# Eight instead of six pieces of the first expert loaded ahead of the ring, and the buffer clearing moved behind the first copy

## The chip, the cores and the metric

The kernel runs on one core of one Trainium2 chip, as one program. The metric is the device time of one execution in microseconds; for the kernel before it is the median of three runs.

## The reference

A decoder trunk of two layers over 256 rows of 1024 float32 values. Layer 0 is latent attention with eight heads and a dense SwiGLU mixer of 2816 columns. Layer 1 is sliding-window attention (16 heads, sinks, a bias by distance) and a mixture of experts. Only the mixture matters for the change:

```python
logits = xn @ w_router                       # 8 experts
top_val, top_idx = lax.top_k(logits, 2)      # each row goes to two of them
hg, hu = xs @ w_gate[e], xs @ w_up[e]        # 1024 x 3584 each
hh = silu(hg) * hu * gate
out += hh @ w_down[e]                        # 3584 x 1024
```

The weights of the eight experts are 8 x 3 x 1024 x 3584 float32 values, 352 MB of the 413 MB that the kernel reads. A final RMS norm follows.

## The kernel before

One block holds a program for each engine. SyncE (SP) issues nearly all weight loads, in one fixed order, into a ring of 28,672 columns in SBUF. In the dense layers the ring is seven slots of 4096 columns. In the mixture it is 16 places (`LAPS`) of one piece each: a piece is 1792 columns (`PIECE`, 896 KB, 128 partitions). An expert has 48 pieces: for each half of its 3584 columns and each of eight k rows one gate and one up piece (m = 0 to 31), then 16 of the down projection (m = 32 to 47), which are loaded in pairs. Piece m lies in place m % 16. Before a load, `room_for` makes SP wait until TensorE has read what lay there. With the first expert these are, for m < 16, the dense weights that the place covers: places of pieces 10 to 12 want the third output product of the attention (`swo_mm` 3), those of 13 and later the fourth. For m = 16 to 31 the count `gu_read` (one per k row that TensorE has read, starting from 1) is waited for, or `gu_mm` for the eighth row of a half. The down pair m = 32, 33 wants the first row of half 1 read.

TensorE takes one item (an expert with its gathered rows) at a time: eight k rows of half 0 (`products(i, 0, k)`), eight of half 1 with transposes and the scatter of the item before between them, the down rows of both halves, and the gather for the next item. An item of at most 64 rows takes the narrow path, one of up to 96 the wide path. The order in which the experts come mixes both. ScalarE (ACT) makes silu of the gate quarters of a half into `sg` (L974), VectorE (DVE) multiplies it with the up quarter into `hh` (L2098), and TensorE begins quarter c of half 1 only when quarter c of half 0 is out of PSUM (`hh_ready`, L1546).

Six pieces of the first expert don't wait for a place in the ring. SP loads them into SBUF that is free before the first item begins: AHEAD_A (m = 30, 31) and AHEAD_B (22, 23) into the end of the arena after the attention's last transposes, and AHEAD_C (26, 27) into xT2 and xT after the router. GpSimd (POOL) copies them into their ring places when these come free (`take_ahead`, L752 to 757, run for B, C, A in this order: the fourth k row of the first half read, the sixth, the eighth). B lies where the transposed hidden values `hhT` are written later, and so ACT waits for both copies of B before it enters its item loop (L1024 to 1025). The places of pieces that come ahead are skipped in SP's order.

Earlier, POOL clears the pads of `slots` and `gates`, and the whole of `ysb`, `sgt` and `hh` (L746 to 750). DVE waits for all five (`cleared`, L1998), and uses the still unused `hh` as scratch room for ranking the experts. After its last copies POOL loads the final gain `gfin` over the room of C (L764).

Of the kernel before, what the change touches and what calls it, by code (L numbers as in the profile page):

```python
# [37 lines left out]
P = 128  # L38
# [12 lines left out]
AH, KVH, HD = 16, 2, 64  # L51
# [8 lines left out]
NE, DFE = 8, 3584  # L60
# [9 lines left out]
ITEMS_MAX = NE * SWEEPS  # L70
# [5 lines left out]
PIECE = HALF_F  # L76
LAPS = 16
# [50 lines left out]
class Semaphores:  # L128
    def __init__(self, sem):
# [120 lines left out]
        self.ahead_loaded_a = sem("ahead_loaded_a")  # L250
        self.ahead_loaded_b = sem("ahead_loaded_b")
        self.ahead_loaded_c = sem("ahead_loaded_c")
        self.gu_read = sem("gu_read")
        self.gu_mm = sem("gu_mm")
        self.sg_ready = sem("sg_ready")
# [21 lines left out]
def build(nc, x, positions, w_in, g_q, g_kv, w_uq, w_ukv, w_o, kv_g, kv_w, kv_b, swa_w_q, swa_b_q,  # L277
          swa_sinks, swa_w_o, swa_b_o, rel_bias, g_attn, g_ffn, f_gate, f_up, f_down, w_router,
          e_gate, e_up, e_down, g_final, consts, out):
    with ExitStack() as ctx:  # L280
# [18 lines left out]
        xT = sb("xT", [P, KD, S])  # L299
        xT2 = sb("xT2", [P, KD, S])  # L300
# [12 lines left out]
        n_items = sb("n_items", [P, 2], I32)  # L313
        wide = sb("wide", [P, ITEMS_MAX], I32)
        order = sb("order", [P, NE], I32)
        ranks = sb("ranks", [P, 8, NE])
        slots = sb("slots", [P, TT, ITEMS_MAX + 1])
        gates = sb("gates", [P, TT, ITEMS_MAX + 1])
# [89 lines left out]
        selg = carve(TT * SLOTS, "p (t n) -> p t n", t=TT)  # L408
        sgt = carve(TT * P, "p (t n) -> p t n", t=TT)
        xgT = carve(KD * SLOTS, "p (k n) -> p k n", k=KD)  # L410
        hh = carve(HALF_F)
        sg = carve(2 * CH, "p (a n) -> p a n", a=2)
        ysb = carve(D)
        early = 12288 - 4 * PIECE
        assert used[0] <= early
        used[0] = early
        hhT = carve(2 * TILES * SLOTS, "p (a j n) -> p a j n", a=2, j=TILES)
        below = hh[:, 0:NE * NE].rearrange("p (a b) -> p a b", a=NE)
        at_place = hh[:, NE * NE:2 * NE * NE].rearrange("p (a b) -> p a b", a=NE)
        terms = hh[:, 2 * NE * NE:5 * NE * NE].rearrange("p (v a b) -> p v a b", v=3, a=NE)  # L420
        gfin = xT2[:].rearrange("p k n -> p (k n)")[:, 0:D]

        AHEAD_B = {LAPS + 6: arena[:, early:early + PIECE], LAPS + 7: arena[:, early + PIECE:early + 2 * PIECE]}
        AHEAD_C = {LAPS + 10: xT2[:].rearrange("p k n -> p (k n)")[:, 0:PIECE], LAPS + 11: xT[:].rearrange("p k n -> p (k n)")[:, 0:PIECE]}
        AHEAD_A = {LAPS + 14: arena[:, early + 2 * PIECE:early + 3 * PIECE], LAPS + 15: arena[:, early + 3 * PIECE:early + 4 * PIECE]}
        assert used[0] <= early + 2 * PIECE

# [180 lines left out]
        @block.sync  # L608
        def _(sp):
            sp.dma_start(h[:, 0, :], x[0, 0:P, :]).then_inc(s.x_loaded0, 16)  # L610
            sp.dma_start(ident, consts[:, C_ID:C_ID + P]).then_inc(s.ident_loaded, 16)
            sp.dma_start(h[:, 1, :], x[0, P:2 * P, :]).then_inc(s.x_loaded1, 16)
            for n, (name, src, k, cols, _, _) in enumerate(stream):
                old = earlier_fill(n, slot_of[n])
                if old is not None:
                    sp.wait_ge(stream[old][4], stream[old][5])
                sp.dma_start(w_of(name), src).then_inc(slot_landed[slot_of[n]], 16)
                if name == "win_q":
                    sp.dma_start(cst[:, C_ID + P:C_N], consts[:, C_ID + P:C_N]).then_inc(s.consts_loaded, 16)

            def piece_of_expert(m, expert):
                kind, half, part = pieces[m]
                if kind == "d":
                    return ed[:, expert, half, part * PIECE:(part + 1) * PIECE]
                return (eg if kind == "g" else eu)[:, expert, part, half * HALF_F:(half + 1) * HALF_F]

            def room_for(i, m, first):

                if m < LAPS:
                    if not first:  # L630
                        sp.wait_ge(s.down_mm, i * (2 * TILES) + (last_down_row(m + 2 * LAPS) + 2 - 2 * TILES))
                        return
                    for sl in dense_under(m):
                        if sl >= 5:
                            sp.wait_ge(*used_up(NU - 1))
                        else:
                            sp.wait_ge(*stream[earlier_fill(DENSE, sl)][4:6])
                    return
                kind, half, k = pieces[m - LAPS]
                if kind == "u":  # L640
                    return
                if k < KD - 1:
                    sp.wait_ge(s.gu_read, i * (2 * KD - 2) + (half * (KD - 1) + k + 2))
                else:
                    sp.wait_ge(s.gu_mm, i * 8 + (4 * half + 5))

            def load_item(i, expert, first):
                for m in range(NP):
                    if first and m == 10:
                        sp.wait_ge(s.spT_mm, AH)  # L650
                        for ma, room in AHEAD_A.items():
                            sp.dma_start(room, piece_of_expert(ma, expert)).then_inc(s.ahead_loaded_a, 16)
                        for ma, room in AHEAD_B.items():
                            sp.dma_start(room, piece_of_expert(ma, expert)).then_inc(s.ahead_loaded_b, 16)
                    if first and m == LAPS:
                        sp.wait_ge(s.swo_mm, 4)
                        sp.wait_ge(s.router_mm, 2)
                        for ma, room in AHEAD_C.items():
                            sp.dma_start(room, piece_of_expert(ma, expert)).then_inc(s.ahead_loaded_c, 16)
                    if first and (m in AHEAD_A or m in AHEAD_B or m in AHEAD_C):  # L660
                        continue
                    room_for(i, m, first)
                    if pieces[m][0] != "d":
                        sp.dma_start(piece(m), piece_of_expert(m, expert)).then_inc(s.piece_landed[m % LAPS], 16)
                    elif m % 2 == 1:
                        _, half, part = pieces[m]
                        sp.dma_start(whole[:, place(m - 1):place(m - 1) + 2 * PIECE],
                                     ed[:, expert, half, (part - 1) * PIECE:(part + 1) * PIECE]).then_inc(s.piece_landed[(m - 1) % LAPS], 16)

            load_item(0, 0, True)  # L670
            sp.wait_ge(s.counts_ready, 1)
            sp.wait_ge(s.order_ready, 1)
            with sp.Fori(1, NE) as i:
                load_item(i, sp.value_load(order[0:1, bass.ds(i, 1)], min_val=0, max_val=NE - 1), False)

            items = sp.value_load(n_items[0:1, 0:1], min_val=NE, max_val=ITEMS_MAX)
            for sweep in range(1, SWEEPS):
                with sp.If(items > sweep * NE):
                    with sp.Fori(0, NE) as e:
                        load_item(e + sweep * NE, sp.value_load(order[0:1, bass.ds(e, 1)], min_val=0, max_val=NE - 1), False)  # L680
                with sp.Else():
                    sp.nop()
            rows = out[0].rearrange("(t p) d -> t p d", p=P)
            sp.wait_ge(s.row_done, 1)
            sp.dma_start(rows[0], xn[:, 0, :]).then_inc(s.out_stored, 16)
            sp.wait_ge(s.row_done, 2)
            sp.dma_start(rows[1][:, 0:512], xn[:, 1, 0:512]).then_inc(s.out_stored, 16)
            sp.wait_ge(s.out_stored, 48)
# [3 lines left out]
        def _(pool):  # L692
# [53 lines left out]
            pool.wait_ge(s.swo_mm, 2)  # L746
            for v in (slots[:, :, ITEMS_MAX:ITEMS_MAX + 1], ):
                nc.gpsimd.memset(v, -1.0).then_inc(s.cleared, 1)
            for v in (gates[:, :, ITEMS_MAX:ITEMS_MAX + 1], ysb[:], sgt[:], hh[:]):
                nc.gpsimd.memset(v, 0.0).then_inc(s.cleared, 1)  # L750
            rstd_rows()
            def take_ahead(rooms, landed, free, count):  # L752
# [3 lines left out]
                for m, room in rooms.items():  # L756
                    nc.gpsimd.tensor_copy(piece(m), room).then_inc(s.piece_landed[m % LAPS], 16)

            take_ahead(AHEAD_B, s.ahead_loaded_b, s.gu_read, 5)
            take_ahead(AHEAD_C, s.ahead_loaded_c, s.gu_read, 7)  # L760
            take_ahead(AHEAD_A, s.ahead_loaded_a, s.gu_mm, 5)
            for m in AHEAD_C:
                pool.wait_ge(s.piece_landed[m % LAPS], 32)
# [9 lines left out]
        def _(act):  # L773
# [247 lines left out]
                act.copy(ysb[NARROW:SLOTS, 512:1024], ps[SLOTS:P, DOWN_BANK, :]).then_inc(s.act_chain, 1)  # L1021
                act.copy(ysb[0:SLOTS, 0:512], ps[0:SLOTS, DOWN_BANK, :]).then_inc(s.y_ready_a, 1)

            for m in AHEAD_B:  # L1024
                act.wait_ge(s.piece_landed[m % LAPS], 32)

            with act.Fori(0, items) as i:
# [640 lines left out]
        def _(dve):  # L1668
# [326 lines left out]
            add_out(3, s.swo_mm, s.h_attn1, SWO_BANK)  # L1995
            evac_hT(1, 1)
            mean_squares(3, 1, D)
            dve.wait_ge(s.cleared, 5)  # L1998
            for q in (s.sel_ready, s.selg_ready, s.hh_ready, s.y_ready_v, s.xgT_ready_v, s.h_added):
                dve.sem_inc(q, 1)  # L2000

            lg, mask, top, idx = (rt[:, :, 8 * n:8 * n + 8] for n in range(4))
# [80 lines left out]
            def dve_item(i, narrow):  # L2083
# [21 lines left out]
                else:  # L2105
                    dve.tensor_copy(ysb[0:NARROW, 512:768], ps[0:NARROW, DOWN_BANK + 1, 0:LASTQ]).then_inc(s.y_last, 1)
                    dve.tensor_copy(ysb[0:NARROW, 768:1024], ps[64:64 + NARROW, DOWN_BANK + 1, 0:LASTQ]).then_inc(s.y_ready_v, 1)

            with dve.Fori(0, items) as i:
                many = dve.value_load(wide[0:1, bass.ds(i, 1)], min_val=0, max_val=1)  # L2110
                with dve.If(many > 0):
                    dve_item(i, False)
                with dve.Else():
                    dve_item(i, True)
# [32 lines left out]
```

## Time and profile before

| | us |
|---|---|
| median of three runs | 1241.17 (1240.88 to 1242.95) |
| the profiled execution | 1240.27 |
| its span | 1238.5 |
| TensorE busy | 1201.4 (97%) |
| VectorE busy | 313.4 (25%) |
| ScalarE busy | 252.4 (20%) |
| GpSimd busy | 40.6 (3%) |

The profile divides the span into 40 slices of 31 us. In the slices from about 433 us on, the mixture, both TensorE and the DMA engines stand at nine tenths or more; before, the DMA engines have slices of three to six tenths. Busy times of TensorE are those of pipelined matmuls with modelled ends. "issue" is time in which an engine waited for nothing that the profile shows. The clock granted to TensorE is given as a share of its full speed.

### The profile page before, as it was taken

What the parts mean: (1) busy time and instruction counts of PE and PEld (TensorE: products, weight loads), DVE (VectorE), ACT (ScalarE), POOL (GpSimd) and SP (SyncE); (2) the same over time, 40 slices, a digit from 0 to 9 for tenths busy, and PEclk for the clock granted to TensorE, in tenths of its full rate; (3) what the DMA queues carried; (4) which work ended last, traced back from release to release, by engine and by line L of the source; (5) the groups of instructions that cost most, each with busy time, mean ns of one, the idle gap of its engine ahead of it and who ended that gap; (6) DMA issues with size and microseconds to landing.
All of it is one profiled execution on the core that took longest, in us unless ns stands there. A gap on an engine that the chain in (4) does not pass through costs nothing.

```text
span 1238.5 us, 20372 instructions
## 1 busy us (share of the span) xinstructions
PE 1201.4 (97%) x8373; PEld 616.4 (50%) x8374; DVE 313.4 (25%) x710; ACT 252.4 (20%) x485; POOL 40.6 (3%) x60
## 2 busy tenths in 40 slices
PE   7999999999999999899999999999999999999996
PEld 4865777778765534334333433443343343334333
DVE  3364676667272311010001002001100100100011
ACT  2252433333263111011021011102101101110111
POOL 2100000000201120000000000000000000000001
PEclk9999999999999999999999999999999999999999
DMA  9613654336635799999999999999999999999994
GB/s 342 231 69 123 217 204 144 129 126 237 241 119 201 318 381 423 419 422 426 419 419 427 418 419 424 422 418 420 427 417 419 426 421 418 423 424 400 421 426 166
DMA packets 73309, 413.19 MB, mean 334 GB/s; under 512 B 6622, under 2 KB 11996, under 8 KB 64780
## 3 DMA queue, kind: packets, MB, share of 16 engines
q1 hardware_dynamic: 71744, 410.41, 81.9%
q8 instruction: 66, 1.08, 0.4%
q0 software_dynamic: 944, 1.29, 0.4%
q10 hardware_dynamic: 540, 0.29, 0.1%
q14 instruction: 15, 0.12, 0.0%
HBM read 410.91 MB, written 1.05 MB: 333 GB/s over the span
## 4 chain that ended last, share of the span: by engine, by line
PE 84%; DMA 7%; DVE 3%; issue 2%; ACT 2%; POOL 0%; ACTq 0%; DVEq 0%; POOLq 0%; SPq 0%
PE ps L1548 19%; PE ps L1528 11%; PE ps L1523 6%; PE ps L1506 6%; PE ps L1620 5%; DMA ring<-in_moe_w_up 4%; PE ps L1221 4%; PE ps L1217 4%; PE ps L1218 4%; PE ps L1510 3%; PE ps L1583 3%; PE ps L1393 2%; PE ps L1603 2%; PE ps L1183 2%; DMA ring<-in_moe_w_down 2%
## 5 line engine op out<-in xcount | busy, mean ns | idle before, releaser
L1548 PE MATMUL ps<-ring,arena 128*64 128x448 f32 x640 | 250.4, 545 | 7.0 <-issue 4.3
L1549 PE MATMUL ps<-ring,arena 128*64 128x448 f32 x640 | 250.5, 545 | 0.0
L1528 PE MATMUL ps<-ring,arena 128*32 128x448 f32 x1152 | 162.1, 539 | 0.0
L1548 PEld LDWEIGHTS ps<-ring,arena 128*64 128x64 f32 x640 | 84.7, 137 | 153.1 <-issue 139.2
L1529 PE MATMUL ps<-ring,arena 128*32 128x448 f32 x384 | 160.0, 539 | 0.0
L1620 PE MATMUL ps<-ring,arena 128*64 128x512 f32 x280 | 124.4, 595 | 0.3 <-DMA ring<-in_moe_w_down 0.3
L1621 PE MATMUL ps<-ring,arena 128*64 128x512 f32 x280 | 124.4, 595 | 0.0
L2098 DVE TENSOR_TENSOR arena<-arena,ps 64x448 f32<-64x448 f32 (+1 forms) x64 | 38.5, 613 | 303.0 <-ACT arena L974 153.6
L1523 PE MATMUL ps<-ring,arena 128*32 128x448 f32 x768 | 91.2, 542 | 5.4 <-DVE arena L2098 4.0
L1528 PEld LDWEIGHTS ps<-ring,arena 128*32 128x32 f32 x1152 | 50.9, 110 | 90.9 <-issue 90.9
L1844 DVE TENSOR_TENSOR w_lo<-ring,w_hi 128x2048 fp32r<-128x2048 f32 x33 | 75.5, 2291 | 60.0 <-ACT w_hi L860 58.6
L1506 PE MATMUL ps<-ring,arena 128*32 128x512 f32 x504 | 87.2, 593 | 0.0
L860 ACT CAST w_hi<-ring 128x2048 fp32r<-128x2048 f32 x33 | 62.9, 1908 | 114.2 <-PE ps L1221 114.2
L1507 PE MATMUL ps<-ring,arena 128*32 128x512 f32 x168 | 86.0, 594 | 0.0
L1549 PEld LDWEIGHTS ps<-ring,arena 128*64 128x64 f32 x640 | 84.8, 137 | 0.0
L1620 PEld LDWEIGHTS ps<-ring,arena 128*64 128x64 f32 x280 | 37.0, 137 | 73.0 <-issue 71.6
L1217 PE MATMUL ps<-w_hi,xT_hi 128*128 128x512 f32 (+1 forms) x192 | 71.6, 380 | 0.0
L1218 PE MATMUL ps<-w_hi,xT_lo 128*128 128x512 f32 (+1 forms) x192 | 70.1, 372 | 0.0
L2080 DVE TENSOR_TENSOR h<-h,ps 128x512 f32<-128x512 f32 x36 | 24.7, 687 | 167.2 <-PE ps L1583 167.2
L985 ACT COPY arena<-ps 128x320 f32<-128x320 f32 (+3 forms) x48 | 21.8, 454 | 207.8 <-PE ps L1603 207.8
L1510 PE MATMUL ps<-ring,arena 128*32 128x256 f32 x672 | 51.7, 379 | 0.0
L1523 PEld LDWEIGHTS ps<-ring,arena 128*32 128x32 f32 x768 | 23.8, 109 | 50.5 <-issue 40.8
(301 smaller groups left out, 1428.7 us busy)
## 6 DMA issues: line engine op xcount, KB each, us to landing
ring<-in_moe_w_down SPq DMA_DIRECT2D x64, 1792.0 KB, 24.2
ring<-in_moe_w_gate SPq DMA_DIRECT2D x125, 896.0 KB, 18.2
ring<-in_moe_w_up SPq DMA_DIRECT2D x125, 896.0 KB, 19.3
ring<-in_ffn_w_gate SPq DMA_DIRECT2D x5, 2048.0 KB, 7.8
ring<-in_ffn_w_up SPq DMA_DIRECT2D x5, 2048.0 KB, 8.2
ring<-in_ffn_w_down SPq DMA_DIRECT2D x5, 2048.0 KB, 7.9
ring<-in_mla_w_o SPq DMA_DIRECT2D x2, 2048.0 KB, 25.6
ring<-in_swa_w_q SPq DMA_DIRECT2D x2, 2048.0 KB, 8.5
```

The source lines that it names most:

```text
L1217: pe.matmul(out, lhs[0][:, k, c], rhs_hi[:, k, :], start=(first and k == 0), stop=False)
L1218: pe.matmul(out, lhs[1][:, k, c], rhs_hi[:, k, :], start=False, stop=False)
L1506: pe.matmul(ps[32 * j:32 * j + 32, bank, :], thirds[j], left, start=first, stop=last)
L1507: pe.matmul(ps[SLOTS:P, bank, :], thirds[2], right, start=first, stop=last)
L1510: mm = pe.matmul(ps[q:q + 32, bank + 1, 0:LASTQ], thirds[j], right[:, cols:cols + LASTQ], start=first, stop=last)
L1523: pe.matmul(ps[q:q + 32, 4 + c // 2, 0:CH], thirds[j], wg[:, (c + e) * CH:(c + e + 1) * CH], start=first, stop=last)
L1528: pe.matmul(ps[32 * j:32 * j + 32, c, 0:CH], thirds[j], wu[:, c * CH:(c + 1) * CH], start=first, stop=last)
L1529: mm = pe.matmul(ps[SLOTS:P, c, 0:CH], thirds[2], wg[:, c * CH:(c + 1) * CH], start=first, stop=last)
L1548: pe.matmul(ps[0:NARROW, c, 0:CH], lhs, wu[:, cols], start=(k == 0), stop=(k == KD - 1))
L1549: mm = pe.matmul(ps[64:64 + NARROW, c, 0:CH], lhs, wg[:, cols], start=(k == 0), stop=(k == KD - 1))
L1620: pe.matmul(ps[0:NARROW, DOWN_BANK, :], lhs, w[:, 0:512], start=first, stop=last)
L1621: mm = pe.matmul(ps[64:64 + NARROW, DOWN_BANK + 1, :], lhs, w[:, 512:1024], start=first, stop=last)
```

## The change

Pieces 24 to 31, the last four k rows of half 1, are now those that come ahead, in four pairs: D (24, 25), B (26, 27), C (28, 29), A (30, 31). Pieces 22 and 23 go through the ring. D lies in the arena from column `HH0`, where `hh`, `sg` and most of `ysb` are later. SP issues it at m = 13, after the attention's eighth product with the values (`spv_mm` 8). POOL takes D first, when the fifth k row is read, waits for its own two copies, clears `hh` and `ysb`, and goes on with B, C and A. ACT waits for the copies of D and of B before its loop, and DVE for the clearing of `hh`. The scratch views for ranking get a tensor of their own.

```diff
+        scratch = sb("scratch", [P, 5 * NE * NE])
...
+        HH0 = used[0]
         hh = carve(HALF_F)
         sg = carve(2 * CH, "p (a n) -> p a n", a=2)
         ysb = carve(D)
+        assert used[0] - HH0 >= 2 * PIECE
...
-        below = hh[:, 0:NE * NE].rearrange("p (a b) -> p a b", a=NE)
+        below = scratch[:, 0:NE * NE].rearrange("p (a b) -> p a b", a=NE)
...
-        AHEAD_B = {LAPS + 6: arena[:, early:early + PIECE], LAPS + 7: arena[:, early + PIECE:early + 2 * PIECE]}
-        AHEAD_C = {LAPS + 10: xT2[:].rearrange("p k n -> p (k n)")[:, 0:PIECE], LAPS + 11: xT[:].rearrange("p k n -> p (k n)")[:, 0:PIECE]}
+        AHEAD_D = {LAPS + 8: arena[:, HH0:HH0 + PIECE], LAPS + 9: arena[:, HH0 + PIECE:HH0 + 2 * PIECE]}
+        AHEAD_B = {LAPS + 10: arena[:, early:early + PIECE], LAPS + 11: arena[:, early + PIECE:early + 2 * PIECE]}
+        AHEAD_C = {LAPS + 12: xT2[:].rearrange("p k n -> p (k n)")[:, 0:PIECE], LAPS + 13: xT[:].rearrange("p k n -> p (k n)")[:, 0:PIECE]}
...
+                    if first and m == 13:
+                        sp.wait_ge(s.spv_mm, AH // 2)
+                        for ma, room in AHEAD_D.items():
+                            sp.dma_start(room, piece_of_expert(ma, expert)).then_inc(s.ahead_loaded_d, 16)
...
-            for v in (gates[:, :, ITEMS_MAX:ITEMS_MAX + 1], ysb[:], sgt[:], hh[:]):
+            for v in (gates[:, :, ITEMS_MAX:ITEMS_MAX + 1], sgt[:]):
                 nc.gpsimd.memset(v, 0.0).then_inc(s.cleared, 1)
...
-            take_ahead(AHEAD_B, s.ahead_loaded_b, s.gu_read, 5)
-            take_ahead(AHEAD_C, s.ahead_loaded_c, s.gu_read, 7)
+            take_ahead(AHEAD_D, s.ahead_loaded_d, s.gu_read, 6)
+            for m in AHEAD_D:
+                pool.wait_ge(s.piece_landed[m % LAPS], 32)
+            nc.gpsimd.memset(hh[:], 0.0).then_inc(s.rows_cleared, 1)
+            nc.gpsimd.memset(ysb[:], 0.0).then_inc(s.y_ready_v, 1)
+            take_ahead(AHEAD_B, s.ahead_loaded_b, s.gu_read, 7)
+            take_ahead(AHEAD_C, s.ahead_loaded_c, s.gu_read, 8)
             take_ahead(AHEAD_A, s.ahead_loaded_a, s.gu_mm, 5)
...
-            for m in AHEAD_B:
+            for m in (*AHEAD_D, *AHEAD_B):
                 act.wait_ge(s.piece_landed[m % LAPS], 32)
...
-            dve.wait_ge(s.cleared, 5)
-            for q in (s.sel_ready, s.selg_ready, s.hh_ready, s.y_ready_v, s.xgT_ready_v, s.h_added):
+            dve.wait_ge(s.cleared, 3)
+            for q in (s.sel_ready, s.selg_ready, s.hh_ready, s.xgT_ready_v, s.h_added):
...
+            dve.wait_ge(s.rows_cleared, 1)
             with dve.Fori(0, items) as i:
```

## Rows read from the trace of the kernel before

**Rows 1.** Page, part 2: DMA engines' busy tenths in 40 slices.
```profile
DMA  9613654336635799999999999999999999999994
```
**Rows 2.** Stretches: us, busy of PE, PEld, DVE, ACT, POOL, PEclk, DMA share, GB/s.
```profile
444.00:445.00 1.00, 1.00 (x8) 0.52 (x5) 0.00 (x0) 0.00 (x0) 0.77 (x2) 1.00 0.35 144
445.00:446.00 1.00, 1.00 (x7) 0.48 (x8) 0.00 (x0) 0.42 (x1) 0.00 (x0) 1.00 0.49 102
...
452.00:500.00 48.00, 48.00 (x242) 19.93 (x242) 6.71 (x13) 5.15 (x13) 0.00 (x0) 1.00 1.01 424
500.00:800.00 300.00, 294.25 (x2162) 115.83 (x2158) 29.44 (x55) 35.45 (x72) 0.00 (x0) 0.99 1.01 422
```
**Rows 3.** Line 664 (gate and up loads), 520 to 1240 us: issue to landing.
```profile
DMA to landing us min/median/max: 11.1/22.2/30.2
```
**Rows 4.** Waits of PE from 500 us on: total, times, longest.
```profile
PE ps L1548 <- issue: 3.3, 1, 3.3
...
PE ps L1523 <- DMA ring<-in_moe_w_up: 1.4, 2, 0.8
```
**Rows 5.** SP's issues in order of time: start, duration, line, target and source.
```profile
395.63 0.43 SPq L664 DMA_DIRECT2D ring<-in_moe_w_gate  x1
402.97 0.33 SPq L664 DMA_DIRECT2D ring<-in_moe_w_up  x1
...
431.78 0.33 SPq L664 DMA_DIRECT2D ring<-in_moe_w_gate  x1
...
437.80 0.33 SPq L664 DMA_DIRECT2D ring<-in_moe_w_gate  x1
...
444.60 0.33 SPq L667 DMA_DIRECT2D ring<-in_moe_w_down  x1
```
**Rows 6.** Line 664, the load issued at 419.8 alone: issue to landing.
```profile
DMA to landing us min/median/max: 5.5/5.5/5.5
```
**Rows 7.** Line 667, the down pair issued at 444.6 alone: issue to landing.
```profile
DMA to landing us min/median/max: 8.7/8.7/8.7
```
**Rows 8.** POOL in order of time, 428 to 445 us.
```profile
428.92 3.29 POOL L757 COPY ring<-arena 128x1792 f32<-128x1792 f32 x2 [21.06 <-PE ps L1549]
434.92 3.30 POOL L757 COPY ring<-xT 128x1792 f32<-128x1792 f32 x2 [2.71 <-PE ps L1549]
...
444.18 0.59 POOL L764 DMA_DIRECT2D xT<-in_g_final  x1
```
**Rows 9.** POOL's groups by shape, 390 to 400 us: busy us, mean ns.
```profile
L750 POOL MEMSET arena<- 128x1792 f32 x1 | 1.6, 1597 | 0.0
L750 POOL MEMSET arena<- 128x1024 f32 x1 | 1.0, 951 | 0.0
```
**Rows 10.** ACT's sequencer, lines 1025 and 971: ns, first and last start us.
```profile
L1025 ACTq EVENT_SEMAPHORE  x1: 17/17/17, 432.2 to 432.2; - x1
...
L971 ACTq FUSED_REGOPS  x1: 47/47/47, 433.2 to 433.2; - x1
```
**Rows 11.** ACT in order of time, 436 to 442 us.
```profile
438.69 1.28 ACT L974 ACT_TABLE_LOAD   x1 [22.12 <-PE ps L1549]
439.99 0.97 ACT L974 ACTIVATE arena<-ps 64x448 f32<-64x448 f32 x2
```
**Rows 12.** The chain that ended last, 436 to 446 us: start, duration.
```profile
440.66 0.62 DVE arena L2098
...
441.33 0.59 PE ps L1548
```
**Rows 13.** PE in order of time, 501 to 512 us.
```profile
506.34 1.00 PE L1548 MATMUL ps<-ring,arena 128*64 128x448 f32 x1 [3.32 <-issue]
...
509.26 0.54 PE L1548 MATMUL ps<-ring,arena 128*64 128x448 f32 x1
509.63 0.54 PE L1548 MATMUL ps<-ring,arena 128*64 128x448 f32 x1
```
**Rows 14.** A stretch of that time, columns as in rows 2.
```profile
507.00:508.00 1.00, 1.00 (x6) 0.35 (x4) 0.00 (x0) 0.00 (x0) 0.00 (x0) 0.50 1.04 430
```

More of the change, by code:

```diff
@@ L252, in __init__ @@
         self.ahead_loaded_c = sem("ahead_loaded_c")
+        self.ahead_loaded_d = sem("ahead_loaded_d")
+        self.rows_cleared = sem("rows_cleared")
         self.gu_read = sem("gu_read")
@@ L417, in build @@
         hhT = carve(2 * TILES * SLOTS, "p (a j n) -> p a j n", a=2, j=TILES)
-        below = hh[:, 0:NE * NE].rearrange("p (a b) -> p a b", a=NE)
-        at_place = hh[:, NE * NE:2 * NE * NE].rearrange("p (a b) -> p a b", a=NE)
-        terms = hh[:, 2 * NE * NE:5 * NE * NE].rearrange("p (v a b) -> p v a b", v=3, a=NE)
+        below = scratch[:, 0:NE * NE].rearrange("p (a b) -> p a b", a=NE)
+        at_place = scratch[:, NE * NE:2 * NE * NE].rearrange("p (a b) -> p a b", a=NE)
+        terms = scratch[:, 2 * NE * NE:5 * NE * NE].rearrange("p (v a b) -> p v a b", v=3, a=NE)
         gfin = xT2[:].rearrange("p k n -> p (k n)")[:, 0:D]
-        AHEAD_B = {LAPS + 6: arena[:, early:early + PIECE], LAPS + 7: arena[:, early + PIECE:early + 2 * PIECE]}
-        AHEAD_C = {LAPS + 10: xT2[:].rearrange("p k n -> p (k n)")[:, 0:PIECE], LAPS + 11: xT[:].rearrange("p k n -> p (k n)")[:, 0:PIECE]}
+        AHEAD_D = {LAPS + 8: arena[:, HH0:HH0 + PIECE], LAPS + 9: arena[:, HH0 + PIECE:HH0 + 2 * PIECE]}
+        AHEAD_B = {LAPS + 10: arena[:, early:early + PIECE], LAPS + 11: arena[:, early + PIECE:early + 2 * PIECE]}
+        AHEAD_C = {LAPS + 12: xT2[:].rearrange("p k n -> p (k n)")[:, 0:PIECE], LAPS + 13: xT[:].rearrange("p k n -> p (k n)")[:, 0:PIECE]}
         AHEAD_A = {LAPS + 14: arena[:, early + 2 * PIECE:early + 3 * PIECE], LAPS + 15: arena[:, early + 3 * PIECE:early + 4 * PIECE]}
@@ L659, in load_item @@
                             sp.dma_start(room, piece_of_expert(ma, expert)).then_inc(s.ahead_loaded_c, 16)
-                    if first and (m in AHEAD_A or m in AHEAD_B or m in AHEAD_C):
+                    if first and (m in AHEAD_A or m in AHEAD_B or m in AHEAD_C or m in AHEAD_D):
                         continue
```

## The prediction, made before the changed kernel was run

> **What bounds the kernel now.** I read the slices first [rows 1]: from the fourteenth or so on the DMA engines are full, and before it they are not. The stretches say the same in numbers [rows 2]: 424 and 422 GB/s at a share of 1.01 from 452 us on, with nothing left to win per byte, but 0.35 and 0.49 in the two microseconds after 444. Then I asked whether the queue runs dry later. It does not: after 520 us no gate or up load landed sooner than 11.1 us after its issue, median 22.2 [rows 3], where one that found the queue empty took 5.5 [rows 6]. So from the first pair of down pieces, issued at 444.60 [rows 5], to the last landing, the DMA engines work without a hole. TensorE is nearly as full, and keeps within a microsecond of them: it waits for a gate or up piece only twice, 1.4 us in all, at most 0.8 [rows 4]. The end is therefore set by when that unbroken stream begins, plus its bytes. TensorE may be late by up to about 0.8 us at those places for nothing.
>
> **The change part by part.**
>
> Bytes. Two more pieces of 896 KB are loaded early. At 422 GB/s a piece takes 2.17 us [rows 2], so 4.3 us of work leave the stretch after 420 us. But which work? The loads issued at 437.80 (28, 29) now come ahead, as do 24 and 25 of 431.78 [rows 5]; 22 and 23 come back, at 428.8. All these lie before the hole, and the next load in SP's order is the down pair, whose place is free only when TensorE has read the first k row of half 1 (444.60). DMA already idles there. Taking 4.3 us away in front of a hole that a wait for room makes only widens it: from about 441 instead of 445. Gain: 0. Every transfer behind the hole is in both kernels. At the other end, if none of the hole counted, it would be the whole 4.3.
>
> The new loads themselves. SP stands waiting between 395.63 and 402.97 [rows 5] for the fourth output product; D is issued in this gap, since the eighth product with the values is ahead of the third output product in TensorE's program. Its two issues (0.43 us each at the row's duration) hide there. They push pieces 13 to 15 and C back by 4.3 us of DMA time, and none is wanted before half 0 reaches its seventh k row near 434.9. Piece 16, issued at 419.76 into an empty queue, has the engines to itself in both kernels. Pieces 22 and 23, now by ring, are the seventh and eighth in that queue: 425.3 + 7 x 2.17 = 440.5. They are read no sooner than three k rows (of 3.0 us, below) after 441.3, at 450. Cost 0.
>
> POOL. This is where I find the price. B's copies began at 428.92 (four k rows read) and C's at 434.92 (six); a k row is 3.0 us, so D's begin at 431.92 (five). Then in order: two copies 3.3 (to 435.2), the clearing of hh 1.6 and of ysb 0.95 [rows 9] (to 437.8, with about 0.1 for the wait on its own copies), and B's two copies 3.3 [rows 8], to 441.2. B's own condition, six rows, was met long before. C's copies follow to 444.5, A's to 447.8; their pieces are the seventh and eighth k row of half 1, read 18 us after it begins, so these hide.
>
> ACT. Before, it passed its wait for B at 432.2 and was ready inside the loop at 433.2 [rows 10]: 1.0 us of register reads and a branch, 5 us ahead of need. The first silu had to wait for TensorE alone: table load at 438.69, silu at 439.99, 1.3 us later [rows 11]. Now the wait ends at 441.2, the loop is entered by 442.2, the table load starts some 0.15 later and the silu at 443.65: 3.65 us late. The table load is behind the same wait and can't be done meanwhile. The chain shows that nothing covers this [rows 11, 12]: silu 439.99, multiply 440.66, first matmul of half 1 at 441.33. TensorE has nothing else in its program there. It restarts at 445.0.
>
> TensorE's clock. Half 0 ends at 440.8 (C's copies at 434.92 plus two k rows, less 0.1 that POOL takes to start); TensorE now stands until 445.0, 4.2 us instead of 0.5. The only comparable stop is at 503: 3.32 us idle, then matmuls at a granted clock of 0.50, which is 1.2 GHz [rows 13, 14]. The four steps from 506.34 to 509.26 took 2.92 us where four at full clock take 4 x 0.37 = 1.5: a loss of 1.4. Bounds for this stop: 0 if the clock doesn't fall, 1.7 if the slow stretch meets it fully. I take 1.4, since this stop is longer. (The Trainium skill, "TensorE: Matmul & The Clock Gate", section "What's actually happening", says that throttled is the default state and activity releases it. By that rule the restart is slow; the rows at 506 agree. With the rule the first down pair is 5.05 us late, without it 3.65.)
>
> DVE. The wait for the cleared hh ends near 436.9, before its first multiply at 440.66: 0. Own scratch room, fewer clears at 393 and one semaphore increment less: all before 411 or beside other work, between -0.1 and 0.1. The first scatter wants ysb only after four k rows of half 1, past 453: 0. I see no cost of copies beside the multiplies: the multiply of 440.66 ran beside a copy in 0.62.
>
> The stream. The down pair is issued at 444.60 + 3.65 + 1.4 = 449.65. Before, it landed 8.7 us after issue [rows 7]; alone it would have taken 5.5 + 2.17 = 7.7, and the 1.0 more went to the gfin load, issued 0.4 us ahead of it [rows 8]. Now gfin goes out at 447.8, 1.9 us ahead, and has most of its bytes through in the hole: I give back 0.9 of the 1.0 at best, nothing at worst. Stream late by 5.05 - 0.9 = 4.15. Without a clock drop the pair goes at 448.25, gfin 0.5 ahead as before, nothing given back: 3.65. Later pairs wait for room on the same late TensorE; their backlog then was small, which could keep up to 0.9 more. TensorE, 5.05 late, loses 0.8 where it used to wait for DMA: 4.25, no more than the stream. The sum lies between 3.65 and 5.05; I take 4.0, between the two clock cases.
>
> Against the profile's own time: span 1238.5 + 4.0 = 1242.5, execution 1240.27 + 4.0 = 1244.3. The median of the runs was 0.9 above the profiled one, so 1241.17 + 4.0 = 1245.2.
>
> **The rivals.**
>
> The stream is shortened (faster). If the early bytes counted, all landings after 450 would come 4.3 us sooner and the time be 1236.9. For it: DMA full for 770 us, and TensorE waiting for it twice. Against: the hole after 444 [rows 2], made by room and not by bytes. It decides only if the down pair finds its place sooner, and nothing makes TensorE read sooner. Between this and nothing lies the 1.0 us of gfin: 1240.2.
>
> The late silu is hidden (no change), 1241.2. For it: TensorE has 0.8 us to spare later and 3.3 us of a stop at 503 [rows 4] that a late start might swallow if it is tied to a time and not to TensorE's position. Against: slack of TensorE doesn't help a DMA stream whose first load is late. It wants DMA to have a second hole, and rows 3 show none.
>
> A deeper loss. The clock falls and stays low longer, and the pairs behind the first keep the whole 5 us or more: 1246.2 to 1247.
>
> **How the numbers follow.** Late silu with a stream 3.6 to 4.4 us later: 0.65. Deeper loss: 0.16. Partly hidden, 1242 to 1244: 0.08. No change: 0.07. Faster: 0.04. From 1242.6 to 1247.2 holds some 0.85 of it. What a measurement can tell from no change is 0.2%, 2.5 us, so slower needs over 1243.65: 0.65 + 0.16 and half of the partly hidden, 0.85; same 0.11; faster 0.04.
>
> **What would show it.** In the changed trace: POOL's order copy x2, memset, memset, copy x6 without a break from 431.9 to 447.8; ACT's table load at 442.3 and not 438.7; TensorE idle some 4 us before the first matmul of half 1, with a granted clock of 0.5 near 445 to 448; the first down load issued at 448 to 450; DMA share near 0 from 441 to 449 apart from gfin, and 1.01 from then on at the same GB/s; the last landing later by what the first down pair was late. Wrong would be: the silu still at 440 (the wait or the order on POOL misread); the silu late and the end unmoved (a hole in the stream that I missed); the first down load near 444.6 with an earlier end (the bytes counted after all).

## The result, and the profile after

The changed kernel takes 1246.34 us, median of seven runs (1244.9 to 1247.63), against 1241.17 (1240.79 to 1242.95, seven runs): ratio 1.004, interval 1.003 to 1.005, 5.2 us slower. The profiled execution took 1247.63 us with a span of 1245.8; it is the slowest of the seven, so the two profiles differ by 7.4 and not 5.2.

POOL in order of time, 425 to 452 us of the changed kernel (start, duration, line):

```profile
433.12 3.29 POOL L767 COPY ring<-arena 128x1792 f32<-128x1792 f32 x2 [24.65 <-PE ps L1564]
436.54 1.59 POOL L772 MEMSET arena<- 128x1792 f32 x1
438.06 0.95 POOL L773 MEMSET arena<- 128x1024 f32 x1
438.96 3.30 POOL L767 COPY ring<-arena 128x1792 f32<-128x1792 f32 x2
442.20 3.30 POOL L767 COPY ring<-xT 128x1792 f32<-128x1792 f32 x2
445.45 3.30 POOL L767 COPY ring<-arena 128x1792 f32<-128x1792 f32 x2
448.70 0.59 POOL L779 DMA_DIRECT2D xT<-in_g_final  x1
```

ACT, and then TensorE, in order of time in the same stretch:

```profile
443.50 1.28 ACT L989 ACT_TABLE_LOAD   x1 [24.67 <-issue]
444.79 0.97 ACT L989 ACTIVATE arena<-ps 64x448 f32<-64x448 f32 x2
...
```

```profile
441.42 0.54 PE L1563 MATMUL ps<-ring,arena 128*64 128x448 f32 x1
...
446.13 1.01 PE L1563 MATMUL ps<-ring,arena 128*64 128x448 f32 x1 [4.17 <-DVE arena L2113]
...
446.94 0.95 PE L1563 MATMUL ps<-ring,arena 128*64 128x448 f32 x1
...
447.68 0.95 PE L1563 MATMUL ps<-ring,arena 128*64 128x448 f32 x1
...
451.42 0.58 PE L1563 MATMUL ps<-ring,arena 128*64 128x448 f32 x1
```

POOL's ten memory operations, eight copies and two clears, now run on without a break, and the first six of them stand in front of the end of ACT's wait for B. (Each matmul of L1563, the up half of a step, has one of L1564, the gate half, beside it; those lines are left out.) The silu comes at 444.79 instead of 439.99 [rows 11]. TensorE stands 4.17 us, and its matmuls then begin every 0.75 us instead of 0.37 until 451.4. SP's issues, and the stretches (columns as in rows 2):

```profile
396.73 0.71 SPq L664 DMA_DIRECT2D arena<-in_moe_w_gate  x1
397.48 0.89 SPq L664 DMA_DIRECT2D arena<-in_moe_w_up  x1
403.59 0.33 SPq L674 DMA_DIRECT2D ring<-in_moe_w_up  x1
...
452.05 0.33 SPq L677 DMA_DIRECT2D ring<-in_moe_w_down  x1
```

```profile
441.00:445.00 4.00, 0.96 (x6) 0.14 (x2) 0.00 (x0) 1.49 (x2) 4.00 (x3) 0.96 0.01 4
445.00:449.00 4.00, 2.87 (x8) 1.00 (x10) 2.29 (x4) 1.84 (x4) 4.00 (x4) 0.50 0.00 0
449.00:453.00 4.00, 4.00 (x17) 1.57 (x15) 0.00 (x0) 0.20 (x1) 0.29 (x1) 0.69 0.38 131
453.00:500.00 47.00, 47.00 (x241) 19.94 (x239) 6.72 (x13) 5.80 (x15) 0.00 (x0) 1.00 1.00 408
500.00:800.00 300.00, 294.39 (x2152) 115.93 (x2148) 29.44 (x55) 34.42 (x68) 0.00 (x0) 0.99 1.01 422
```

D's loads hide in SP's gap. The first down pair goes out at 452.05 instead of 444.60, after 8 us in which the DMA engines move almost nothing (share 0.01, then 0.00). From 500 us on everything is as before: 1.01 and 422 GB/s, at a new offset. From 415 us on TensorE waits even less for gate and up pieces than in [rows 4]: once, 0.2 us.

Part of the 7.45 us between the two issues isn't the change's. The first product of item 0 starts at 417.69 here and at 416.49 in the profile of before; its start lies between 415.15 and 418.04 over all thirteen profiles of this study, in both kinds of kernel. So I count from that start. The down products of the two kernels, with the start of the first and the last of them:

```profile
L1620 PE MATMUL ps<-ring,arena x280: 592/592/644, 472.7 to 1224.8; 128*64 128x512 f32 x140
```

```profile
L1635 PE MATMUL ps<-ring,arena x280: 592/592/644, 480.1 to 1232.1; 128*64 128x512 f32 x140
```

Before: first down load 444.60 - 416.49 = 28.1 us after the start, last down product 1224.8 - 416.5 = 808.3. Changed: 34.4 and 814.4. The load is 6.3 late, the end 6.1. The same for all kernels, with the medians:

| kernel | silu | first down load | last down product | median, and of before beside it |
|---|---|---|---|---|
| before | 23.5 | 28.1 | 808.3 | |
| the change | 27.1 | 34.4 | 814.4 | 1246.34, 1241.17 |
| the change again | 27.1 | 34.1 | 814.4 | 1246.02, 1240.84 |
| B's wait later | 23.5 | 28.1 | 809.1 | 1241.71, 1242.26 |
| clears behind B | 24.8 | 29.4 | 809.5 | 1241.97, 1242.26 |
| ysb behind B | 26.2 | 32.5 | 812.5 | 1245.72, 1241.70 |
| kept busy | 27.1 | 31.7 | 811.8 | 1243.59, 1240.84 |
| before, ACT late | 28.7 | 34.9 | 815.1 | 1247.39, 1242.26 |
| four ahead | 23.5 | 28.1 | 809.4 | 1241.89, 1242.26 |
| eight, better order | 22.2 | 27.3 | 807.7, 807.5 | 1240.80, 1241.70; 1240.33, 1240.84 |
| six, same repairs | 22.2 | 27.3 | 807.7 | 1240.99, 1241.70 |
| primed alone | 22.2 | 27.3 | 808.7 | 1241.89, 1241.70 |

The columns are us from the start of item 0's first product to: the first silu, the issue of the first down pair, the start of the last down product. The end comes 780.0 to 781.4 us after the first down load in every row; it takes the longest, 781.0 to 781.4, in B's wait later, four ahead and primed alone. Each offset is from one profile. Against the one profile of before (1240.27, 0.9 under its median) the ends are 0.1 to 1.7 us later than the medians say, in all rows but the second run of the better order. So that profile was probably a short execution, also behind item 0's start; a single profile can't show it.

### The profile page after: what moved, and what is told of

Read it like the earlier page. It is cut to its first block, busy times and chain, and to the rows that moved or that the text cites. A ratio compares the mean times of both kernels' runs of the same rounds, so it can differ in the third digit from the quotient of the medians.

```text
span 1245.8 us, 20376 instructions
## 1 busy us (share of the span) xinstructions
PE 1207.1 (97%) x8373; PEld 615.5 (49%) x8374; DVE 313.6 (25%) x710; ACT 252.4 (20%) x485; POOL 43.7 (4%) x62
## 4 chain that ended last, share of the span: by engine, by line
PE 88%; DVE 3%; DMA 3%; issue 2%; ACT 2%; POOL 1%; ACTq 0%; POOLq 0%; DVEq 0%
PE ps L1563 19%; PE ps L1543 10%; PE ps L1635 9%; PE ps L1521 6%; PE ps L1538 5%; PE ps L1236 4%; PE ps L1232 4%; PE ps L1233 4%; PE ps L1525 3%; PE ps L1598 3%; PE ps L1618 3%; PE ps L1512 3%; PE ps L1408 2%; PE ps L1198 2%; DMA ring<-in_moe_w_up 2%
## 5 line engine op out<-in xcount | busy, mean ns | idle before, releaser
L1563 PE MATMUL ps<-ring,arena 128*64 128x448 f32 x640 | 254.7, 552 | 9.5 <-DVE arena L2113 6.3
L1564 PE MATMUL ps<-ring,arena 128*64 128x448 f32 x640 | 254.8, 553 | 0.0
L1563 PEld LDWEIGHTS ps<-ring,arena 128*64 128x64 f32 x640 | 85.8, 139 | 158.3 <-issue 140.9
L1543 PEld LDWEIGHTS ps<-ring,arena 128*32 128x32 f32 x1152 | 48.0, 110 | 93.6 <-issue 93.6
L1564 PEld LDWEIGHTS ps<-ring,arena 128*64 128x64 f32 x640 | 86.0, 139 | 0.0
L2095 DVE TENSOR_TENSOR h<-h,ps 128x512 f32<-128x512 f32 x36 | 24.8, 688 | 169.8 <-PE ps L1598 169.8
L1538 PEld LDWEIGHTS ps<-ring,arena 128*32 128x32 f32 x768 | 22.5, 110 | 50.7 <-issue 41.5
```

The lines of the kernel that those rows point to most:

```text
L1538: pe.matmul(ps[q:q + 32, 4 + c // 2, 0:CH], thirds[j], wg[:, (c + e) * CH:(c + e + 1) * CH], start=first, stop=last)
L1543: pe.matmul(ps[32 * j:32 * j + 32, c, 0:CH], thirds[j], wu[:, c * CH:(c + 1) * CH], start=first, stop=last)
L1563: pe.matmul(ps[0:NARROW, c, 0:CH], lhs, wu[:, cols], start=(k == 0), stop=(k == KD - 1))
L1564: mm = pe.matmul(ps[64:64 + NARROW, c, 0:CH], lhs, wg[:, cols], start=(k == 0), stop=(k == KD - 1))
```

## The experiments

### The wait for B taken out of the way

```diff
-            for m in (*AHEAD_D, *AHEAD_B):
+            for m in AHEAD_D:
                 act.wait_ge(s.piece_landed[m % LAPS], 32)
...
+                    if half == 0:
+                        for m in AHEAD_B:
+                            act.wait_ge(s.piece_landed[m % LAPS], 32)
                     for n in range(3):
                         hhT_evac(i, half, n, narrow)
```

> The changed kernel with ACT's wait for the copies of B taken from ahead of its item loop to ahead of the first transposed hidden values; it waits for D alone before the loop. Theory (the late silu makes the loss, and the early bytes are worth nothing): first silu back at about 440, first down load at about 444.6 to 445.2, time within 1 us of before, 1240.2 to 1242.2. Rival 1 (the two more pieces do shorten the stream once nothing else is late): 1236.9. Rival 2 (the loss comes from D itself, its room, loads or copies, not from the wait): still 1244 to 1247.

1241.71 us (1240.56 to 1242.49) against 1242.26 of before beside it, ratio 0.9998 (0.9989 to 1.0007). ACT, and SP:

```profile
438.25 1.28 ACT L989 ACT_TABLE_LOAD   x1 [21.06 <-PE ps L1567]
439.54 0.97 ACT L989 ACTIVATE arena<-ps 64x448 f32<-64x448 f32 x2
```

```profile
444.15 0.33 SPq L677 DMA_DIRECT2D ring<-in_moe_w_down  x1
```

With the start at 416.04 both stand exactly where before has them: silu 23.5 after it, down load 28.1. All the rest of the change is in this kernel. The bytes that are gone from the ring's queue only widen the hole in front of the down load, as two of its stretches show:

```profile
439.00:440.00 1.00, 1.00 (x8) 0.29 (x4) 0.00 (x0) 0.99 (x3) 1.00 (x1) 1.00 0.06 22
...
443.00:444.00 1.00, 1.00 (x6) 0.14 (x2) 0.00 (x0) 0.00 (x0) 1.00 (x2) 1.00 0.00 0
```

In before the DMA share was still 0.95 from 443 to 444 us. So the loss hangs on this wait, and the bytes gained nothing that the interval (1.1 us to either side) would show: 1236.9 is excluded.

### The clears behind B's copies

```diff
-            nc.gpsimd.memset(hh[:], 0.0).then_inc(s.rows_cleared, 1)
-            nc.gpsimd.memset(ysb[:], 0.0).then_inc(s.y_ready_v, 1)
             take_ahead(AHEAD_B, s.ahead_loaded_b, s.gu_read, 7)
+            nc.gpsimd.memset(hh[:], 0.0).then_inc(s.rows_cleared, 1)
+            nc.gpsimd.memset(ysb[:], 0.0).then_inc(s.y_ready_v, 1)
```

> The changed kernel with the clearing of hh and ysb put behind the copies of B instead of ahead of them, so that B is copied 2.6 us sooner. Theory: B copied by 438.5, silu at about 441.0, 1.0 us late, TensorE stands 1.5 us, its clock stays; the down load 1.0 late: 1241.6 to 1243.0. Rival (the clock falls or not with the mere order, the size of the delay being secondary): 1245 or more. Rival (bytes): 1237.9.

1241.97 (1241.39 to 1242.83), ratio 0.9997 (0.9988 to 1.0006). TensorE's wait, and a stretch behind it:

```profile
PE ps L1563 <- DVE arena L2113: 1.8, 1, 1.8
```

```profile
444.00:446.00 2.00, 2.00 (x12) 0.74 (x12) 1.14 (x2) 0.49 (x1) 2.00 (x2) 1.00 0.00 0
```

The silu is 1.3 us late, TensorE stands 1.8 us at full clock, and in the trace the down load is 1.3 late and the end 1.2; in the runs this small a loss doesn't show, and is 0.7 us at most by the interval. That is less than the 1.0 us that I expected. The rival with a fallen clock is out.

### Only the clearing of ysb behind B

```diff
             nc.gpsimd.memset(hh[:], 0.0).then_inc(s.rows_cleared, 1)
-            nc.gpsimd.memset(ysb[:], 0.0).then_inc(s.y_ready_v, 1)
             take_ahead(AHEAD_B, s.ahead_loaded_b, s.gu_read, 7)
+            nc.gpsimd.memset(ysb[:], 0.0).then_inc(s.y_ready_v, 1)
```

> The changed kernel with only the clearing of ysb (0.95 us) put behind the copies of B. Silu 2.7 us late, TensorE stands some 3.3 us, as long as at 503, where the clock fell. Theory (delay plus clock): if the clock falls for 3.4 us or more, stream 2.7 + 1.4 or more late, 3.5 to 5 us over before; if it stays up, 1.5 to 2.7 over. Rival (in proportion to the delay alone, no clock): 1.5 to 2.7 over before in all runs, and one level of times.

1245.72 (1245.08 to 1246.32), ratio 1.0033 (1.0021 to 1.0045): 4.0 us. Stretches of this kernel:

```profile
445.00:446.00 1.00, 1.00 (x4) 0.35 (x6) 0.84 (x2) 1.00 (x2) 1.00 (x2) 0.60 0.00 0
446.00:448.00 2.00, 2.00 (x8) 0.73 (x6) 0.69 (x2) 0.04 (x1) 2.00 (x2) 0.50 0.00 0
448.00:449.00 1.00, 1.00 (x6) 0.32 (x4) 0.00 (x0) 0.00 (x0) 0.95 (x2) 0.69 0.00 0
```

The silu is 2.7 us late and TensorE stands 3.3 us, until 444.91. Its clock falls 0.3 us after it has started again, and is low for 3.4 us; in the changed kernel it is low for 6.8. The down load is 4.4 late. Against the kernel with both clears behind B the silu is 1.4 us later and the down load 3.1; in the runs the two kernels lie some 4 us apart, each with an interval of over 1 us to either side. The loss is not in proportion to the delay: 1.7 us of the 3.1 are matmuls at half pace. That the clock fell is read from one profile; the six runs, all 3.4 us or more over the median of before beside them (1241.70), fit it, and none is at the 1.5 to 2.7 that the expectation gave for a clock that stays up.

### TensorE kept busy while it waits

```diff
+                    if k == 0 and half == 1 and c == 0:
+                        with pe.If(i < 1):
+                            for _ in range(4):
+                                keep_busy(5, 512)
```

> The changed kernel, with four matmuls on constants (some 0.86 us each, into a bank that nobody reads) that TensorE runs in the first item alone, between half 0 and the wait for the first quarter of half 1. ACT and POOL are as late as in the changed kernel, but TensorE stands some 0.7 us instead of 4.2. Theory (the loss is the late silu plus the slow clock after the standstill): clock stays at full, first down load 3.6 to 4 us late instead of 6 to 7, stream 3.5 late: 2 to 3 us under the changed kernel run beside it. Rival (the loss beyond the late silu is something else, a restart of the DMA queue or of the ring): within 0.7 us of the changed kernel.

1243.59 (1242.18 to 1245.31, 11 runs), ratio 1.0020 (1.0011 to 1.0029); the changed kernel beside it 1246.02. TensorE:

```profile
442.24 3.70 PE L1464 MATMUL ps<-cst 128*128 128x512 f32 x8
446.49 0.59 PE L1569 MATMUL ps<-ring,arena 128*64 128x448 f32 x1 [0.54 <-DVE arena L2119]
...
446.91 0.54 PE L1569 MATMUL ps<-ring,arena 128*64 128x448 f32 x1
...
447.29 0.54 PE L1569 MATMUL ps<-ring,arena 128*64 128x448 f32 x1
```

The four matmuls on constants, whose result nobody reads, are the eight records of the first line. The silu is as late as in the changed kernel (27.1), and POOL's order the same. Matmuls follow every 0.37 us, and the down load is 3.6 late instead of 6. So, by the medians, 2.4 us of the 5.2 are the clock's, and 2.75 the late silu's. The highest run here (1245.31) lies under the lowest of the changed kernel (1245.44); the size of the 2.4 is known to about 2 us, by the two intervals.

### The change again

> The changed kernel as it is, beside the others on the same chip: 4 to 5.5 us over before, with the clock at 1.2 GHz for 3.4 or 6.8 us from about 444 us on. Rival (the first result was in part the chip or the day): under 3 us over before.

1246.02 (1245.44 to 1246.73), ratio 1.0043 (1.0029 to 1.0057): 5.2 us, as the first time. TensorE stands 4.18 us, and six steps of its matmuls and part of a seventh go at half pace, for 4.8 us.

### Before, with ACT late and nothing else

```diff
-            for m in AHEAD_B:
+            for m in (*AHEAD_B, LAPS + 14):
                 act.wait_ge(s.piece_landed[m % LAPS], 32)
```

> The kernel before, six pieces as they were, with nothing but one more wait of ACT ahead of its loop: for the first copy of A, which ends at 442.6. Theory: silu at about 445.05, 5.05 us late; first down load 5 to 8 us late with the clock at 1.2 GHz for a stretch; 1246 to 1249. Without a fall of the clock 1245.5. Rival (the loss of the change comes from D's loads and copies, or from 7 to 8 us less of DMA work in the right place): under 1243.

1247.39 (1246.91 to 1248.12), ratio 1.0042 (1.0029 to 1.0056). Its waits of PE from 415 us on:

```profile
PE ps L1548 <- DVE arena L2098: 7.9, 5, 5.7
```

Six pieces, no D, no late clears, and a loss as soon as ACT is late: silu 5.2 late, down load 6.8, end 6.8 in the trace, 5.1 us in the runs. This is the other half of the proof: a late ACT is sufficient. It isn't a copy of the changed kernel, since the silu is later than there (5.2 against 3.6) for the same loss in the runs; of TensorE's slow time, 442.7 to 449.5, about half lies in the standstill, and the matmuls lose 1.7 us by it instead of 2.7.

### Four pieces ahead

```diff
-        AHEAD_C = {LAPS + 10: xT2[:].rearrange("p k n -> p (k n)")[:, 0:PIECE], LAPS + 11: xT[:].rearrange("p k n -> p (k n)")[:, 0:PIECE]}
+        AHEAD_C = {}
...
-            take_ahead(AHEAD_C, s.ahead_loaded_c, s.gu_read, 7)
```

> The kernel before with pair C (26, 27) not ahead but by its turn through the ring: four pieces ahead instead of six. Theory (a hole of 2 to 3.4 us stands between the last of half 1 and the first down pair, which the 4.3 us more fill first): stream late by 4.3 less the hole, 1 to 2.3 us: 1242.2 to 1243.5. Rival (each piece counts in full): 1245.5. Rival (no piece counts): 1241.2.

1241.89 (1240.42 to 1243.35), ratio 0.9999 (0.9990 to 1.0008). Two stretches, and the landing of the first down pair, issued at 445.73:

```profile
444.00:446.00 2.00, 2.00 (x13) 0.81 (x10) 0.23 (x1) 0.00 (x0) 1.90 (x2) 1.00 1.00 416
446.00:448.00 2.00, 2.00 (x14) 0.98 (x15) 0.00 (x0) 0.42 (x1) 0.00 (x0) 1.00 1.00 416
```

```profile
DMA to landing us min/median/max: 10.6/10.6/10.6
```

Here the hole of [rows 2] is filled: from 444 us on the queue doesn't empty. The pair lands 1.9 later after its issue than in [rows 7], and the end is 1.1 late in the trace, 0.4 us under before in the median. I had expected 1 to 2.3 us over it. So even the third pair ahead is worth 1.0 us at most, by the upper end of the interval, where 4.3 us of transfer were moved.

### The silu table and a better order

Three repairs on eight pieces: ACT's wait for B later; a silu of one column at the head of each item, so that the table is loaded before TensorE's count is waited for; and in POOL's order gfin right behind C's copies, which come before B's (C holds pieces 26, 27 and B 28, 29).

```diff
             def act_item(i, narrow):
+                act.activation(primed[:], vecT[:, 0:1], ACT.Silu)
...
             nc.gpsimd.memset(hh[:], 0.0).then_inc(s.rows_cleared, 1)
-            nc.gpsimd.memset(ysb[:], 0.0).then_inc(s.y_ready_v, 1)
-            take_ahead(AHEAD_B, s.ahead_loaded_b, s.gu_read, 7)
-            take_ahead(AHEAD_C, s.ahead_loaded_c, s.gu_read, 8)
-            take_ahead(AHEAD_A, s.ahead_loaded_a, s.gu_mm, 5)
+            take_ahead(AHEAD_C, s.ahead_loaded_c, s.gu_read, 7)
             for m in AHEAD_C:
                 pool.wait_ge(s.piece_landed[m % LAPS], 32)
             pool.dma_start(gfin, g_final.rearrange("(a n) -> a n", a=1).to_broadcast([P, D])).then_inc(s.rel_loaded, 16)
+            nc.gpsimd.memset(ysb[:], 0.0).then_inc(s.y_ready_v, 1)
+            take_ahead(AHEAD_B, s.ahead_loaded_b, s.gu_read, 8)
+            take_ahead(AHEAD_A, s.ahead_loaded_a, s.gu_mm, 5)
...
```

(The edit of ACT's wait is the one of the first experiment.)

> Eight pieces ahead, with three repairs: ACT waits for B later (as in the run before); the silu table is loaded ahead of the wait for TensorE, by a silu of one column at the head of each item; and POOL's order is D, clear hh, C, the gfin load, clear ysb, B, A, so that gfin falls into the hole of the DMA queue. Theory: first silu at about the time of its condition (438.6 by the clock of before) instead of 1.3 us later, half 1 begins 0.5 sooner, gfin takes nothing from the first down pair (1.0 before, 2.4 in the run with B's wait later): stream 0.5 to 1.5 us sooner than before: 0.5 to 1.5 us under before. Rival (TensorE is the bound as soon as the stream is sooner, with 0.8 us to give): at most 0.8 under. Rival (nothing left here): equal to before within 0.5.

> Eight pieces with the three repairs once more, to narrow its interval. Theory (the stream starts some 1 us sooner against the start of the first item): 0.5 to 1.3 us under before. Rival (no gain): 0.3 under to 0.3 over.

1240.80 (1239.60 to 1242.65) against 1241.70, ratio 0.9991 (0.9982 to 1.0000); again 1240.33 (1239.48 to 1241.29) against 1240.84, ratio 0.9996 (0.9987 to 1.0005). ACT:

```profile
437.56 1.28 ACT L1023 ACT_TABLE_LOAD   x1 [18.59 <-POOL ring L768]
438.85 0.20 ACT L1023 ACTIVATE primed<-vecT 128x1 f32<-128x1 f32 x1
440.04 1.19 ACT L990 ACTIVATE arena<-ps 64x448 f32<-64x448 f32 x2 [0.99 <-PE ps L1569]
```

> The kernel before with its six pieces, the table load ahead of the wait as in the kernel beside it, and gfin loaded behind the copies of C instead of A. Theory (two more pieces ahead are worth nothing): as fast as the eight-piece kernel beside it, within 1 us, so 0 to 1.5 under before; gfin now runs beside the loads of 28 and 29 and pushes the start of the down pair by at most 1 us. Rival (the hole that the eight pieces widen is of use once other work fills it): 1 us or more slower than the eight-piece kernel.

The kernel before with the silu primed and gfin behind C: 1240.99 (1239.65 to 1242.15), ratio 0.9997 (0.9988 to 1.0006).

> Eight pieces, B's wait later, and the silu table loaded ahead of the wait; POOL's order as in the changed kernel. Theory: silu 1.3 us sooner than in the same kernel without it, half 1 begins 0.5 sooner, the stream 0.5 sooner: 0 to 0.7 under before. Rival (the table load is not on the path): as without it.

B's wait later and the silu primed alone, on eight pieces: 1241.89 (1239.4 to 1243.04), ratio 1.0003 (0.9994 to 1.0012). That is 0.2 us over before and not 0 to 0.7 under it, as I had expected.

In the traces of the better order and of the same repairs on six pieces the silu is 1.3 us sooner, the down load 0.8 and the end 0.6 to 0.8. The better order is faster than the change by 5 us, and perhaps than before by 0.5 to 0.9; the interval of the second measurement holds 1.0, so that isn't shown. Where gfin stayed behind A (primed alone, B's wait later), its load falls between the first two down pairs, and the end comes some 1 us later after the first of them. The expectation of the better order has gfin take 2.4 us from the first pair with B's wait later; the trace shows otherwise: that pair landed 6.8 us after its issue, sooner than in before (8.7), and the one behind it 9.6.

## Why the prediction was right, and which terms were off

**The bound.** Right: an unbroken stream whose start sets the end. The offset of the first down load and that of the last product go together in all rows of the table, within 1.4 us, and the rates behind 500 us are equal. TensorE's room beside the stream was larger than the 0.8 us that I gave it: its waits for DMA from 415 us on are 0.2 us in all in the changed kernel and 2.6 in before with ACT late, and both start the last product 780.0 to 780.2 us after the first down load.

**The bytes.** Right at 0, within about 1 us, shown by the kernel with B's wait later, by eight pieces beside six with the same repairs, and from the other side by the one with four pieces: the places, not the bytes, decided when the down loads could go.

**POOL and ACT.** Counted from item 0's start the silu is 3.6 us late (3.65 forecast), TensorE stands 4.17 (4.2), POOL's chain from the first copy to the gfin load takes 15.6 us (15.9). That ACT's wait was the price of the change is shown by taking it away, which leaves no loss over 0.9 us by the interval, and by making ACT late in the kernel before.

**The clock.** The term that was mis-sized. It fell, as taken, but I gave it the 1.4 us of the stop at 503. Here seven steps took 446.13 to 451.42 = 5.3 us, which at 0.375 are 2.6: a loss of 2.7. The upper bound of 1.7, half of the 3.4 us for which the clock was low around 506, was also too low: here it was low for 6.8 us, from 444.7 to 451.5, and the slow stretch went on for most of a k row after the restart. The mistake was to take the price from one stop. The stop at 503, behind item 0, is in all thirteen profiles, 3.2 to 3.5 us long, and its price differs: in five of them the clock stays full behind it and nothing is lost, in three the first eight steps lose 1.4 to 1.7 us (before is one of these), in five 2.7 to 3.0. With B's wait later and in the changed kernel the first matmul behind it is:

```profile
506.09 0.58 PE L1566 MATMUL ps<-ring,arena 128*64 128x448 f32 x1 [3.52 <-issue]
```

```profile
513.66 1.00 PE L1563 MATMUL ps<-ring,arena 128*64 128x448 f32 x1 [3.19 <-issue]
```

The longer stop is the one that left the clock up. One profile of before couldn't show that range. In the runs the clock is worth 2.4 us (kept busy against the change). (The Trainium skill, "TensorE: Matmul & The Clock Gate", section "What's actually happening", has throttled as the default and activity as what releases it; the trace agrees, 0.50 after 4.17 us of standing and full clock when four matmuls filled them; but in five of the thirteen profiles TensorE stood for 3.2 to 3.5 us behind item 0 without a fall.)

**What gfin gives back.** Wrong in its reason. The first pair did land sooner after its issue, 7.1 us instead of 8.7 [rows 7] (and 8.5 in the kernel kept busy, where gfin goes out 0.7 us ahead of it); the next pair gave it back. Issued 3.91 us after the first, it took 9.1:

```profile
DMA to landing us min/median/max: 7.1/7.1/7.1
```

```profile
DMA to landing us min/median/max: 9.1/9.1/9.1
```

(first pair, second pair of the changed kernel). From the issue of the first to the landing of the second are 13.0 us, and 13.1 in before (3.9 + 9.2), where gfin runs beside them. So in the traces the give-back of 0.9 was 0.1. Why the second pair takes that long I can't say.

**The sum.** With 3.6 + 2.7 - 0.1 = 6.2 the trace's 6.1 is met. The medians have 5.2. That the profile of before was a short one would account for the 0.9 between them; it isn't shown. The forecast of 4.0 took the middle of two clock cases, 3.65 and 4.15, where the case that happened is 6.1 in the trace; the range, 1242.6 to 1247.2, held because of the deeper-loss rival. That rival as written (clock low for longer, nothing given back by the pairs behind) is what happened, and 0.16 was too little for it. The sum with a fallen clock, 4.15, is 2 us short of the traces; that the median, 1246.34, came within 1.2 us of the forecast of 1245.2 is in part luck, since the runs show 0.9 less than the traces.

## What to carry to other kernels

A load that is moved ahead is worth something only if the queue behind it can start sooner; where the next load waits for room, look at what frees the room, and not at the bytes. When work is put into an in-order queue, here D's two copies and two clears on POOL, ahead of B's copies, count its time up to every wait of another engine on anything behind it. A standstill of TensorE should be priced with what a fallen clock costs behind it, or filled. Here 1.8 us of standing cost nothing more, stops of 3.2 to 3.5 us cost between 0 and 3.0 us on top, and so the price is a range and not a number; 3.6 us of late silu cost 5.2 in the runs, and four matmuls on constants brought 2.4 back.

## What I had not expected of the hardware

A standstill of 1.8 us left the clock up. After 4.2 us of standing it was still at half for 5.4 and 4.8 us, in the two profiles of the changed kernel; it had fallen 2.7 and 2.2 us into the stop. The cost doesn't grow with the stop: the longest, 5.7 us (before, ACT late), lost 1.7 us behind it, less than those of 4.2 us with 2.7 and 2.4. With only the clearing of ysb behind B the clock fell when TensorE was already at work again, 0.3 us after a stop of 3.3. And the same stop behind item 0, 3.2 to 3.5 us, cost 0, 1.4 to 1.7 or 2.7 to 3.0 us from one kernel's profile to the next. There it leaves no mark on the end: the kernel with B's wait later loses nothing and starts its last product 781.0 us after its first down load, the changed kernel loses 3.0 and does so after 780.0. What goes instead are TensorE's waits for DMA from 415 us on, 3.2 us in the one and 0.2 in the other.

The start of item 0 scatters over 2.9 us between profiles, half of what was to be measured. Offsets from it agree within 0.1 us for the end of the two profiles of the changed kernel, where their spans differ by 2.2; against before they still lie 0.9 above the medians.
